# Two-block transformer kernel: the order of splits and of matmul passes at the edges of the first block

## What is computed

```
h = rms_norm(x);  u = h @ w_in;  four branches (state space, three attentions), gated and summed
x = x + rms_norm(merged @ w_out)
h = rms_norm(x);  x = x + rms_norm((silu(h @ w_g) * (h @ w_up)) @ w_down)
```

## Time and profile before

| | us |
|---|---|
| median of 3 runs | 2224.13 (2223.38 to 2224.67) |
| the profiled execution's own time | 2225.01 |
| its span (first to last instruction) | 2222.9 |

### The profile page before, as it was taken

One profiled execution on the slowest core, in us unless ns is written; L12 is line 12 of the kernel. 1 busy time (PEld: TensorE's weight loads), 2 busy tenths in 40 slices (PEclk: granted clock), 3 DMA queues, 4 the chain that ended last, 5 costly groups with the idle time before them and its releaser, 6 DMA issues. The chain is left out here.

```text
span 2222.9 us, 35593 instructions
## 1 busy us (share of the span) xinstructions
PE 2187.2 (98%) x15408; PEld 1982.1 (89%) x15408; DVE 1458.8 (66%) x1616; ACT 1115.5 (50%) x1423; POOL 48.4 (2%) x46
## 2 busy tenths in 40 slices
PE   8999999999999999999999999999999999999998
PEld 7999998888899999788789999888888999988887
DVE  5778567555768756656677867456657786744664
ACT  4555644454564564545465445444446553544443
POOL 0000000000000000000000000000000000000000
PEclk9999999999999999999999999999999999999999
DMA  7545565565654555556545445456655544445553
GB/s 233 171 146 167 152 199 171 189 200 189 180 177 145 149 180 184 170 189 229 178 134 136 150 134 171 139 168 200 204 175 155 150 135 143 161 158 165 189 201 112
DMA packets 280483, 376.90 MB, mean 170 GB/s; under 512 B 22400, under 2 KB 224198, under 8 KB 280327
## 3 DMA queue, kind: packets, MB, share of 16 engines
q1 hardware_dynamic: 280326, 374.62, 53.8%
HBM read 368.10 MB, written 1.05 MB: 166 GB/s over the span
## 5 line engine op out<-in xcount | busy, mean ns | idle before, releaser
L1305 DVE TENSOR_TENSOR a_wlo<-a_ring,a_whi 128x2048 fp32r<-128x2048 f32 (+1 forms) x173 | 393.0, 2274 | 101.9 <-ACT a_whi L1035 101.2
L3233 DVE TENSOR_TENSOR b_wlo<-b_ring,b_whi 128x2048 fp32r<-128x2048 f32 (+1 forms) x168 | 379.6, 2263 | 110.9 <-ACT b_whi L2906 110.4
L1035 ACT CAST a_whi<-a_ring 128x2048 fp32r<-128x2048 f32 (+1 forms) x173 | 328.1, 1900 | 137.9 <-PE ps L921 48.7
L2906 ACT CAST b_whi<-b_ring 128x2048 fp32r<-128x2048 f32 (+1 forms) x168 | 317.4, 1890 | 154.4 <-PE ps L2881 79.0
L611 PE MATMUL ps<-a_nsp,a_whi 128*128 128x256 f32 x2144 | 387.3, 283 | 0.0
L611 PEld LDWEIGHTS ps<-a_nsp,a_whi 128*128 128x128 f32 x2144 | 334.1, 192 | 0.2
L611 PE MATMUL ps<-a_nsp,a_wlo 128*128 128x256 f32 x1072 | 306.3, 286 | 0.0
L2272 PE MATMUL ps<-b_nsp,b_whi 128*128 128x256 f32 x1568 | 284.7, 283 | 0.0
L2272 PEld LDWEIGHTS ps<-b_nsp,b_whi 128*128 128x128 f32 x1568 | 244.0, 191 | 0.1
L2272 PE MATMUL ps<-b_nsp,b_wlo 128*128 128x256 f32 x784 | 227.9, 291 | 0.9 <-DVE b_wlo L3233 0.9
L611 PEld LDWEIGHTS ps<-a_nsp,a_wlo 128*128 128x128 f32 x1072 | 205.5, 192 | 1.6 <-issue 1.0
(11 more groups left out here) (584 smaller groups left out, 4092.6 us busy)
## 6 DMA issues: line engine op xcount, KB each, us to landing
a_ring<-in_w_in SPq DMA_DIRECT2D x49, 1024.0 KB, 5.4
b_ring<-in_w_in SPq DMA_DIRECT2D x46, 1024.0 KB, 6.0
a_ring<-in_w_ffn_in SPq DMA_DIRECT2D x44, 1024.0 KB, 5.1
a_ring<-in_w_gate SPq DMA_DIRECT2D x32, 1024.0 KB, 5.5
b_ring<-in_w_up SPq DMA_DIRECT2D x32, 1024.0 KB, 5.4
b_ring<-in_w_down SPq DMA_DIRECT2D x32, 1024.0 KB, 4.9
a_ring<-in_w_ffn_out SPq DMA_DIRECT2D x22, 1024.0 KB, 5.0
a_ring<-in_w_branch SPq DMA_DIRECT2D x16, 1024.0 KB, 5.1
```

What stands on the lines that cost most here:

```text
L1035: nc.scalar.copy(part(whi, h), part(ring, h)).then_inc(hi_ok, 1)
L1305: nc.vector.tensor_tensor(part(wlo, h), part(ring, h), part(whi, h).bitcast(F32), ALU.subtract).then_inc(lo_ok, 1)
L2906: nc.scalar.copy(part(whi, h), part(ring, h)).then_inc(hi_ok, 1)
L3233: nc.vector.tensor_tensor(part(wlo, h), part(ring, h), part(whi, h).bitcast(F32), ALU.subtract).then_inc(lo_ok, 1)
```

## The change

On **ACT**, the two casts of tile 0 now stand before the cast of the second weight part instead of after it (FFN edges, lead edge, first cq edge). On **DVE**, the two subtractions of tile 0 now stand before the first weight part's subtraction instead of after it (the same four edges). On **PE**, each lead part takes its eight matmuls with the high weight part first, for which it waits for `hi_ok` instead of `lo_ok`, and then waits for `lo_ok` and takes the four with the low weight part (all five edges). The transposes of tile 1 stay where they were at the cq edges; at the others they now stand after the second of the four low-weight matmuls of part 2. The number of instructions that compute stays the same.

```diff
--- before.py
+++ after.py
@@ -625,9 +625,21 @@
 
         def lead_rows(i, t):
             hi, lo = part(whi, i), part(wlo, i)
+            if prior is not None:
+                b, r = ps[:, i // 2 * 2 + t, :], 4 * (i % 2)
+                for kk in range(4):
+                    k = r + kk
+                    for j, x_ in enumerate((nlo, nhi)):
+                        T.matmul(b, x_[:, k, t * P:(t + 1) * P], hi[:, kk, :], start=k == 0 and j == 0, stop=False)
+                if t == 0:
+                    pe.wait_ge(lo_ok, i + 1)
+                for kk in range(4):
+                    if i == 2 and t == 0 and kk == 2:
+                        turn_in(pe.engine, l, 1)
+                    k = r + kk
+                    mm = T.matmul(b, nhi[:, k, t * P:(t + 1) * P], lo[:, kk, :], start=False, stop=k == KD - 1)
+                return mm
             for kk in range(4):
-                if prior is not None and i == 2 and t == 0 and kk == 2:
-                    turn_in(pe.engine, l, 1)
                 if prior is None and i == 0 and t == 0 and kk == 2:
                     pe.wait_ge(lo_ok, 1)
                 k = 4 * (i % 2) + kk
@@ -645,7 +657,7 @@
                         if t == 0 and prior is None and i == 0:
                             pe.wait_for(first_lo, 1)
                         elif t == 0:
-                            pe.wait_ge(lo_ok, i + 1)
+                            pe.wait_ge(lo_ok if prior is None else hi_ok, i + 1)
                         if i < 2:
                             pe.wait_ge(nlo_ok, 2 * t + i + 1)
                         mm = lead_rows(i, t)
@@ -952,14 +964,20 @@
             h = H_FIN + j
             hi, lo = part(whi, h), part(wlo, h)
             if t == 0:
-                pe.wait_ge(lo_ok, h + 1)
+                pe.wait_ge(hi_ok, h + 1)
             if j < 2:
                 pe.wait_ge(nlo_ok, 4 + 2 * t + j + 1)
             for kk in range(4):
                 k = 4 * (j % 2) + kk
-                for n, (x_, w) in enumerate(((nlo, hi), (nhi, lo), (nhi, hi))):
-                    mm = T.matmul(ps[:, 4 * t + j // 2, :], x_[:, k, t * P:(t + 1) * P], w[:, kk, :],
-                                  start=k == 0 and n == 0, stop=k == KD - 1 and n == 2)
+                for n, x_ in enumerate((nlo, nhi)):
+                    T.matmul(ps[:, 4 * t + j // 2, :], x_[:, k, t * P:(t + 1) * P], hi[:, kk, :],
+                             start=k == 0 and n == 0, stop=False)
+            if t == 0:
+                pe.wait_ge(lo_ok, h + 1)
+            for kk in range(4):
+                k = 4 * (j % 2) + kk
+                mm = T.matmul(ps[:, 4 * t + j // 2, :], nhi[:, k, t * P:(t + 1) * P], lo[:, kk, :],
+                              start=False, stop=k == KD - 1)
                 if j == 2 and t == 0 and kk == 1:
                     turn_tile(pe.engine, l, 1, 1)
             if t == 1:
@@ -1257,8 +1275,8 @@
         mix_squares(0)
         x_squares(0)
         hi(H_FIN)
+        hi_tile(act.engine, l, 1, 0)
         hi(H_FIN + 1)
-        hi_tile(act.engine, l, 1, 0)
         mix_squares(1)
         hi(H_FIN + 2)
         x_squares(1)
@@ -1292,8 +1310,8 @@
         down_squares(0)
         following.square_in(act.engine, following.layer, 0, ends(l).x[0])
         hi(H_END)
+        following.hi_in(act.engine, following.layer, 0)
         hi(H_END + 1)
-        following.hi_in(act.engine, following.layer, 0)
         down_squares(1)
         hi(H_END + 2)
         following.square_in(act.engine, following.layer, 1, ends(l).x[1])
@@ -1671,10 +1689,9 @@
             if t == 1:
                 lo(H_FIN + 2)
             norm_x(t, 2 * t + 3)
+            lo_tile(dve.engine, l, 1, t)
             if t == 0:
                 lo(H_FIN)
-            lo_tile(dve.engine, l, 1, t)
-            if t == 0:
                 lo(H_FIN + 1)
         for i in range(H_FIN + 2, H_END - 1):
             if i == H_FIN + 2:
@@ -1719,10 +1736,9 @@
             if t == 1:
                 lo(H_END + 2)
             following.scale_in(dve.engine, following.layer, t)
+            following.lo_in(dve.engine, following.layer, t)
             if t == 0:
                 lo(H_END)
-            following.lo_in(dve.engine, following.layer, t)
-            if t == 0:
                 lo(H_END + 1)
 
     def gpsimd(pool, l, prior, following):
@@ -2298,13 +2314,19 @@
         def cq_rows(h, t):
             hi, lo = both(h)
             if t == 0:
-                pe.wait_ge(lo_ok, h + 1)
+                pe.wait_ge(hi_ok, h + 1)
             pe.wait_ge(nlo_ok, 2 * t + h + 1)
             for kk in range(4):
                 k = 4 * h + kk
-                for n, (w, x_) in enumerate(((hi, nlo), (lo, nhi), (hi, nhi))):
-                    mm = T.matmul(ps[:, 2 + t, 0:384], x_[:, k, t * P:(t + 1) * P], w[:, kk, :],
-                                  start=k == 0 and n == 0, stop=k == KD - 1 and n == 2)
+                for n, x_ in enumerate((nlo, nhi)):
+                    T.matmul(ps[:, 2 + t, 0:384], x_[:, k, t * P:(t + 1) * P], hi[:, kk, :],
+                             start=k == 0 and n == 0, stop=False)
+            if t == 0:
+                pe.wait_ge(lo_ok, h + 1)
+            for kk in range(4):
+                k = 4 * h + kk
+                mm = T.matmul(ps[:, 2 + t, 0:384], nhi[:, k, t * P:(t + 1) * P], lo[:, kk, :],
+                              start=False, stop=k == KD - 1)
             if h == CQB:
                 mm.then_inc(cq_ps, 1)
             elif t == 1:
```

## The result

The changed kernel takes **2226.93 us** (median of 20 runs, 2225.64 to 2228.16), the kernel before 2223.49 (median of 20, 2222.33 to 2224.77). The ratio is 1.0016, with a 95% interval of 1.0010 to 1.0023: slower by 3.4 us, within the 0.2% that was called no change, and on the side that was forecast. The forecast was 2226.4, from a median of 2224.13 before that rested on three runs; with 20 it is 2223.49. The difference is off by 1.1 us (3.4 for 2.3); that the absolute number is off by 0.5 only is luck.

The account below looks back on a forecast made before the run. PE was taken as the bound (busy 2187.2 of 2222.9 us), with DVE's chain setting the FFN edges. FFN edges 0.60, lead 0.32, first cq 1.40, second cq -0.05 sum to +2.3 us: 2224.13 to 2226.4, range 2222.8 to 2230.2.

Parts of the forecast that it names:

- The chain on DVE: At an FFN edge, DVE's gapless work up to tile 1's scaling sets the end; forecast 0.79 us longer.
- D: Lengthening of DVE's chain at an edge: 0.79 us at inner edges (bounds 0.73 and 1.02), 1.40 at the first cq edge.
- The inner edges: The two FFN edges and the lead edge: +0.30 us per FFN edge, +0.32 at the lead edge.
- ACT's part: Tile 0's casts before hi(F1) on ACT: costs nothing; without it DVE's wait would be longer.
- The pass order: PE's high-weight passes first: gives at most 0.49 us at an inner edge before the transposes bind.
- The first cq edge: There the chain's lengthening counts whole: tile 1's first matmul +1.40 us later, PE's wait growing from 3.88 to about 5.3.
- the lower bound's case: At the first cq edge the clock's rise keeps its place, so later rows win 0.7 us back: +0.7.
- The second cq edge: Only PE's order changes there; its 0.94 us wait moves in front of the transposes: -0.05 us, at most -0.1.
- The rule weighed: ACT's and DVE's queues are strictly first in, first out: +2.3 us stands; if DVE could pass waiting instructions, -1.5.
- the further fall: Rival: the clock also falls at an FFN, lead or second cq edge, about 3.0 us a fall; chance 0.23.
- The stalls: Rival: PE's waits of 0.84 and 1.62 us really go at three edges, -7.4 us to 2216.8; chance 0.06.
- the hand-offs: Rival: tile hand-offs between PE, ACT and DVE are quicker than assumed, down to 2222.6 us; chance 0.08.

Follow-up runs that it names:

- the dose: The changed kernel, but ACT keeps both weight casts ahead of tile 0's casts; 2230.89 us against 2223.12 for the kernel before, ratio 1.0038.
- cq restored: The changed kernel, but with ACT's and DVE's old order at the first cq edge; 2225.64 us against 2223.12 for the kernel before, ratio 1.0010.
- half cover: The changed kernel, but at the inner edges the first low part is subtracted half before, half after tile 0's subtractions; 2225.15 us against 2224.32 for the kernel before.
- the low parts later: The kernel before with PE's new order, and lo(1), lo(2) moved later on DVE at the first cq edge; 2221.47 us against 2224.32, again 2221.17 against 2223.45.
- the turn by halves: The low parts later, plus each four transposes at both cq edges waiting only for the half they read; 2220.10 us against 2223.45 for the kernel before.
- queues alone: The kernel before with only the new order on ACT and DVE, PE's passes as before; 2226.91 us against 2223.12, ratio 1.0017.

## Why the prediction was right

- **The chain on DVE.** Right. D was put at 0.79 and measured at 0.86 (12.97 - 12.11). Nearly all of the missing 0.07 is in front of the pair: the first subtraction starts 367.24 - 365.92 = 1.32 us after the transposes do, where I took 1.26 from tile 1. From its start to the next instruction it is 368.51 - 367.24 = 1.27, for 1.26 forecast.
- **The inner edges.** Forecast +0.30 and +0.32 at tile 1's first matmul; measured (380.95 - 365.12) - (381.84 - 366.35) = +0.34. Up to the next edge +0.46 to +0.53. The term left out is the 0.13 us that PE loses after a wait.
- **ACT's part.** Shown by the dose: without that move D goes from 0.86 to 2.13.
- **The pass order.** Right as a limit: it gives 0.49 less the toll, whatever D is.
- **The first cq edge.** Forecast +1.40 at tile 1's first matmul, measured +1.45. Bounded at +0.7 to +2.1 for what the clock would give back or take: +0.82 by the next edge. That is the lower bound's case, not the middle that I took: the clock rose 20.8 us after the scaling of tile 0 before and 21.1 us after the change, so it kept its place and gave 0.6 back in this execution. The stand of 5.3 us came out at 4.86, because 0.43 of it moved in front of lo(0).
- **The second cq edge.** Forecast -0.05, measured -0.07 from scaling to transposes (10.59 to 10.52).
- **The rule weighed.** DVE stands 0.71 us with lo(F0)'s inputs ready: program order, as the rows of before already said.
- **Rivals.** The granted clock of the changed kernel is 1.00 up to 2220 us but for the first cq edge, so the further fall did not happen in its profiled execution. It did at the same lead edge in cq restored, so it belongs to this order in some executions. Its price at an inner edge was put too high: about 3 us forecast, 1.0 to 1.3 measured, because the stretch there was 3.4 us and not 10.2. The stalls did not really go, and the hand-offs were no quicker.
- **The signs.** The gaps of DVE came (0.71 and 1.37 us), and the scalings moved apart as said. Two signs fell short: the wait for b_xm is 4.86, not over 5, and PE's waits at an FFN edge sum to 2.23 us, not to more than 2.5. Neither touches the chain on DVE.
- **The size.** Forecast +2.3, measured +3.4 (interval +2.2 to +5.1). The edges of the profile sum to 0.46 + 0.53 + 0.51 + 0.82 - 0.10 = 2.2, taking 0.51 for FFN 1 where the load was on time; the toll at the inner edges is 0.4 of what I had left out. In the profiled executions the rest cancels: the late load gave +1.0, and the kernel's start, before the first edge, -1.23. The medians have some 1 us more than the sum, and the recorded clocks say where it most likely is. In the profiled executions a mean granted clock of 0.998 went with 6.8 us at 0.50 up to 2200 us, 0.997 with 10.2 and 0.996 with 13.7. The kernel before, run again beside the experiments, on three chips, has 0.998 in 51 of 68 runs (median 2223.38) and 0.997 in 17 (2224.57); its profiled execution, 2225.01, is of the second kind and slower than any of its first 20 runs. The changed kernel has 0.997 in 15 of 20 (2226.67) and 0.996 in 5 (2227.87). At 0.997 for both the change costs 2.1 us, close to the forecast; the rest of the 3.4 is that the changed kernel runs at the lower clock for longer in most executions, which the forecast had only as a rival with a higher price. The clocks are rounded and the chips differ, so this is a reading and not shown.

## What to carry to other kernels

Ahead of reordering a queue, ask whether the instruction moved to its head is ready. If it isn't, what stood there was its cover, and the wait is added to the whole chain. Find the engine that has no gap in the critical stretch and count only its length; the waits of the busiest engine move about without telling it. Where one profile is compared with another, look at the granted clock in both first: here it moved one edge by up to 3 us with the same or nearly the same order. Half of the old head instruction can be cover enough, and a wait on exactly the half that is read is a cheap gain.

## What the runs showed of the hardware

- PE's stands of 1.85 and 1.14 us with four matmuls between were followed by 1.2 GHz in one kernel; stands of 1.41, 0.47 and 1.08 us were not, in the one execution profiled. Stands of 1.10 and 0.53 us (cq restored, lead edge) and of 0.99 and 0.46 us (half cover, FFN 1) were followed by 3.4 us at 1.2 GHz; like stands at the other inner edges of the same kernels were not. One profile without a fall doesn't show that an order is safe.
- A fall costs half of the time for which tile 1's rows run at 1.2 GHz: some 2.0 us of 4.1 at the first cq edge of the low parts later, against the turn by halves (3.1 less the 1.1 by which the transposes came sooner). At an inner edge the 3.4 us at 1.2 GHz cost 1.0 to 1.3 us, and next to nothing where PE had a wait behind them (queues alone).
- In three of the ten profiled executions a load of 1 MB of w_ffn_out was late enough to cost PE 1.0 us, far from any change.
